# A hybrid trunk layer on one core: x is transposed unnormalised, and its norm is moved to the weights and to V

## The reference, cut to what matters

```
def rmsnorm(x, g):
    return x * rsqrt(mean(x*x, -1) + EPS) * g          # EPS = 1e-6
u   = rmsnorm(h, mix_norm_g)
qkv = u @ wqkv                                         # (1024, 1536)
q, k, v = split(qkv)
q = rmsnorm(q, gq); k = rmsnorm(k, gk)                 # per head, over 64
scores = q k^T / 8 - slope*dist, masked to 128 back, softmax with a sink
h = h + (probs @ v) @ wo
h = h + square(relu(rmsnorm(h, mlp_norm_g) @ w1)) @ w2
h = h + sigmoid(rmsnorm(h, ple_norm_g) @ w_gate) * (p @ w_proj)
```

## Time and profile before

| | us |
|---|---|
| median of 3 runs | 1136.48 (1136.44 to 1138.27) |
| profiled execution | 1134.62 |
| its span | 1132.8 |
| first score product of block 0 starts | 37.03 |
| distance of two blocks in the steady part | 32.77 |
| start of the first product with wo | 270.72 |

### The profile page before, as it was taken

How to read it: one execution, slowest core, us unless ns; L and a number is a source line. 1 busy time by engine, 2 the same in 40 slices (tenths; PEclk the granted TensorE clock), 3 DMA queues, 4 the chain that set the end, 5 groups by cost and what they waited for, 6 DMA issues and landing times.

```text
span 1132.8 us, 15063 instructions
## 1 busy us (share of the span) xinstructions
PE 1102.8 (97%) x5418; PEld 925.4 (82%) x5418; DVE 766.1 (68%) x1170; ACT 453.1 (40%) x796; POOL 116.3 (10%) x191
## 2 busy tenths in 40 slices
PE   7899999998999999899999999999999999999998
PEld 5788888886888887688888888888888888888887
DVE  5788887888553579866776677588778773564311
ACT  5566666666432323223313324453333332243100
POOL 6531332323100000000000000000000000010000
PEclk9999999999999999999999999999999999999999
DMA  7000000004143304433443234999888882111211
GB/s 279 21 19 19 19 19 19 19 26 161 38 141 101 131 18 167 190 126 137 179 167 130 112 142 139 371 413 340 286 297 284 288 279 75 38 38 56 84 44 41
DMA packets 61801, 154.41 MB, mean 136 GB/s; under 512 B 5040, under 2 KB 6064, under 8 KB 61744
## 3 DMA queue, kind: packets, MB, share of 16 engines
q1 hardware_dynamic: 61600, 153.12, 37.8%
q10 hardware_dynamic: 144, 0.52, 0.1%
HBM read 119.55 MB, written 34.08 MB: 136 GB/s over the span
## 4 chain that ended last, share of the span: by engine, by line
PE 80%; DVE 10%; issue 3%; ACT 3%; POOL 2%; DMA 0%; ACTq 0%; DVEq 0%; POOLq 0%
PE pair L2023 24%; PE pair L2003 21%; PE pair L2066 8%; PE pair L1884 7%; PE pair L1756 5%; PE pair L2043 4%; PE pair L1961 3%; ACT probs L859 2%; PE pair L1824 2%; PE pair L2079 2%; PE pair L1795 2%; DVE probs L1260 2%; DVE probs L1278 1%; PE pair L1931 1%; PE pair L1807 1%
## 5 line engine op out<-in xcount | busy, mean ns | idle before, releaser
L2023 PE MATMUL pair<-uT 128*128 128x512 f32 x1176 | 266.7, 389 | 0.0
L2023 PEld LDWEIGHTS pair<-uT 128*128 128x128 f32 x1176 | 220.7, 188 | 45.8
L1086 ACT ACTIVATE uT<-wo_raw 128x1024 fp32r<-128x1024 f32 x63 | 64.3, 1054 | 105.2 <-PE pair L2023 90.3
L1577 DVE TENSOR_TENSOR uT<-wo_raw,uT 128x1024 fp32r<-128x1024 f32 x63 | 74.9, 1221 | 38.8 <-ACT uT L1086 38.8
L1756 PE MATMUL pair<-WA,xT 128*128 128x512 f32 x384 | 95.7, 398 | 1.7 <-DVE kn L1217 0.9
L1884 PE MATMUL pair<-WA,oT 128*128 128x512 f32 x384 | 91.8, 397 | 2.3 <-DVE WA L1336 1.7
L1884 PEld LDWEIGHTS pair<-WA,oT 128*128 128x128 f32 x384 | 72.3, 191 | 17.7 <-issue 1.9
L859 ACT ACTIVATE probs<-probs,nmax 128x257 f32<-128x257 f32 x128 | 63.8, 501 | 52.2 <-DVE nmax L1265 52.0
L1756 PEld LDWEIGHTS pair<-WA,xT 128*128 128x128 f32 x384 | 69.7, 188 | 18.0 <-issue 3.1
L643 POOL TENSOR_SCALAR row_var<-row_ssq 128x1 f32<-128x1 f32 x24 | 4.6, 192 | 718.5 <-ACT hn L987 712.2
L2003 PE MATMUL pair<-WA,WB 128*128 128x512 f32 x312 | 72.8, 389 | 3.3 <-DVE RES L1537 3.3
(11 more groups left out here) (181 smaller groups left out, 1949.6 us busy)
## 6 DMA issues: line engine op xcount, KB each, us to landing
wo_raw<-in_m_w SPq DMA_DIRECT2D x53, 512.0 KB, 6.4
wo_raw<-hid_kept SPq DMA_DIRECT2D x36, 512.0 KB, 4.6
hid_kept<-RES SPq DMA_DIRECT2D x28, 512.0 KB, 2.6
emb<-in_m_w SPq DMA_DIRECT2D x20, 512.0 KB, 6.1
RES<-in_m_w SPq DMA_DIRECT2D x8, 1024.0 KB, 6.5
RES<-in_a_wqkv SPq DMA_DIRECT2D x12, 512.0 KB, 8.9
uT_f<-in_m_w SPq DMA_DIRECT2D x6, 1024.0 KB, 6.7
act_buf<-hid_kept SPq DMA_DIRECT2D x11, 512.0 KB, 4.4
```

What stands on the lines that cost most here:

```text
L1086: nc.scalar.activation(operand(t, which, HI), unit(t, which), ACT.Copy).then_inc(op_hi, 1)
L1577: nc.vector.tensor_tensor(operand(t, which, LO), unit(t, which), operand(t, which, HI).bitcast(F32), ALU.subtract).then_inc(op_ready, 1)
L2023: mm = nc.tensor.matmul(ps[4 * (j % 2) + m][:], operand(t, 0, s)[:, k, m * P:(m + 1) * P], operand(t, 1, r)[:, k, :], start=(g == 0 and k ...
```

## The change

1. x is transposed as it lands. `x_norm` on DVE is gone, and `turn_x` waits for the DMA of x and reads xb. The next load of x waits for the transposes and for the squares.
2. The channel weights are multiplied into wqkv when it is split. The gain is loaded as 8 rows of 128 numbers (instead of 128 copies of 1024), turned by one PE transpose and copied by DVE into mix_col. `hi_unit` and `lo_unit` of the units 0 to 11 are each two instructions of 128x512 with a per-partition scale instead of one of 128x1024.
3. The row factor is applied in `stage_v` (as ACT's scale). For q and k it is left out, and POOL adds one instruction per block (row_eps) so that the EPS in `head_norm` keeps its meaning.
4. `x_squares` and POOL's `x_norm` are for block n+1 and not n+2: the squares stand at the end of ACT's j = 0, POOL's row factor ahead of `head_norm("q0", n + 1)`.
5. The start is in another order, below. Ten units have a place of their own (two of them in ring), so only units 10 and 11 wait for a place. The 34 + 8 warm-up transposes are 11 + 11 + 11.

```
@@ sp
             def load_x(b):
-                sp.wait_ge(xn_ready, b)
+                sp.wait_ge(xT_done, 2 * b)
+                sp.wait_ge(x_squared, b)
...
-                if u >= 8:
-                    sp.wait_ge(w_split, u - 8 + 1)
+                if u >= 10:
+                    sp.wait_ge(w_split, u - 10 + 1)
...
@@ gpsimd
+            pool.memset(gain[:, 0:P], 0.0).then_inc(gain_zero, 1)
...
+            def x_norm(b):
+                stand(pool, x_squared, b + 1)
+                pool.tensor_scalar(row_var[:], row_ssq[:], 1.0 / D, EPS, ALU.mult, ALU.add).then_inc(x_var, 1)
+                pool.wait_ge(x_var, b + 1)
+                pool.tensor_tensor(row_rstd[:], row_var[:], half[:, 0:1], ALU.pow).then_inc(x_rstd, 1)
+                pool.tensor_scalar(row_eps[:], row_var[:], EPS, 1.0, ALU.mult, ALU.mult).then_inc(x_eps, 1)
+                stand(pool, x_eps, b + 1)
...
-            row_norm(x_squared, x_var, x_rstd, 0)
...
+            x_norm(0)
             for h in range(H):
-                if h == 10:
+                if h == 4:
                     head_norm("k", 0)
+                if h == 9:
+                    head_norm("q0", 0)
                 bias_of(h, slice(P, 2 * P), bias_first)
-            head_norm("q0", 0)
-            row_norm(x_squared, x_var, x_rstd, 1)
...
                 if not last:
+                    x_norm(n + 1)
                     head_norm("q0", n + 1)
-                if x_too and not last:
-                    row_norm(x_squared, x_var, x_rstd, n + 2)
@@ scalar
+                    act.wait_ge(mix_ready, 1)
+                    act.wait_ge(wqkv_in(u)[0], 16 * (u // 10 + 1))
+                    for i in range(2):
+                        last_half = nc.scalar.activation(split_to(kind, k, HI)[:, i, :], raw_wqkv(u)[:, i, :], ACT.Copy,
+                                                         scale=mix_col[:, 2 * k + i:2 * k + i + 1])
...
-                    if j == 1 and x_too:
-                        x_squares(n + 2)
+                    if j == 0 and not last:
+                        x_squares(n + 1)
...
-            act.dma_start(gain[:], mix_g.partition_broadcast(P)).then_inc(gain_in, 16)
+            act.wait_ge(gain_zero, 1)
+            act.dma_start(gain[0:KT, 0:P], mix_g.rearrange("(k p) -> k p", p=P)).then_inc(gain_in, 16)
...
-            x_squares(0)
-            hi_unit(0, "kv", 0)
             xT_hi_half(0, 0)
             xT_hi_half(0, 1)
+            hi_unit(0, "kv", 0)
             hi_unit(1, "kv", 1)
+            x_squares(0)
...
-            hi_unit(9, "q8", 1)
             act.wait_ge(scales_ready, 1)
             k_hi_part(0)
+            hi_unit(9, "q8", 1)
+            part_squares("q0", 0)
             hi_unit(10, "q8", 2)
-            part_squares("q0", 0)
             hi_unit(11, "q8", 3)
-            x_squares(1)
@@ vector
+                    for i in range(2):
+                        last_half = nc.vector.scalar_tensor_tensor(
+                            out=dst[:, i, :], in0=raw_wqkv(u)[:, i, :], scalar=mix_col[:, 2 * k + i:2 * k + i + 1],
+                            in1=top[:, i, :].bitcast(F32), op0=ALU.mult, op1=ALU.subtract)
...
-                            dve.wait_ge(bias_first, 1 + H)
+                            dve.wait_ge(bias_first, 1 + G * (j + 1))
...
-            dve.wait_ge(gain_in, 16)
-            x_norm(0)
-            lo_unit(0, "kv", 0)
+            dve.wait_ge(mix_turned, 1)
+            nc.vector.tensor_scalar(mix_col[:], ps[3][:, 0:KT], 1.0, None, ALU.mult).then_inc(mix_ready, 1)
             xT_lo_half(0, 0)
             xT_lo_half(0, 1)
+            lo_unit(0, "kv", 0)
...
             lo_unit(6, "q0", 2)
+            head_scale("k", 0)
             lo_unit(7, "q0", 3)
-            head_scale("k", 0)
...
             lo_unit(10, "q8", 2)
+            head_scale("q0", 0)
             lo_unit(11, "q8", 3)
-            head_scale("q0", 0)
-            x_norm(1)
@@ tensor
-                pe.wait_ge(xn_ready, b + 1)
+                pe.wait_ge(x_in, 16 * (b + 1))
...
-            warm_up(WARM_UP)
+            def turn_mix():
+                pe.wait_ge(gain_in, 16)
+                nc.tensor.transpose(ps[3][:, 0:P], gain[:, 0:P], ident[:]).then_inc(mix_turned, 1)
+            warm_up(WARM_UP // 3)
+            turn_mix()
+            warm_up(WARM_UP // 3)
             turn_x(0)
-            warm_up(WARM_UP // 4)
+            warm_up(WARM_UP // 3)
```

More of the change, by code:

```diff
@@ L135, in trunk_layer @@
         rden = sb("rden", [P, 2, G], F32)
-        sb("to_line", [P, 56], F32)
+        mix_col = sb("mix_col", [P, KT], F32)
+        row_eps = sb("row_eps", [P, 1], F32)
+        sb("to_line", [P, 47], F32)
         in_a = ExitStack()
@@ L255, in row_kept @@
         def row_kept(b):
-            return 16 * ((U_W1 - b + 7) // 8 + 1)
+            return 16 * (3 if b < 2 else 2)
         units = []
@@ L320, in trunk_layer @@
         x_rstd = sem("x_rstd")
-        xn_ready = sem("xn_ready")
+        x_eps = sem("x_eps")
+        gain_zero = sem("gain_zero")
+        mix_turned = sem("mix_turned")
+        mix_ready = sem("mix_ready")
         xT_done = sem("xT_done")
@@ L429, in split_to, with wqkv_in, raw_wqkv @@
                     "proj": lambda: wp_s[:, s, k, :]}[kind]()
+        def wqkv_in(u):
+            return (ring_in[u - 8] if u in (8, 9) else row_moved[u % 10], 16)
+        def raw_wqkv(u):
+            return (ring[:, u - 8, :] if u in (8, 9) else RES[:, u % 10, :]).rearrange("p (k n) -> p k n", k=2)
         def shaped(raw, like):
@@ L645, in row_norm @@
                 pool.tensor_tensor(row_rstd[:], row_var[:], half[:, 0:1], ALU.pow).then_inc(rstd_sem, 1)
+            def x_norm(b):
[5 more added lines that the diff above has]
+                stand(pool, x_eps, b + 1)
             def head_norm(X, b):
                 stand(pool, summed[X], b + 1)
-                pool.tensor_scalar(var[X][:], ssq[X][:], 1.0 / HD, EPS, ALU.mult, ALU.add).then_inc(var_ready[X], 1)
+                pool.tensor_scalar(var[X][:], ssq[X][:], 1.0 / HD, row_eps[:], ALU.mult, ALU.add).then_inc(var_ready[X], 1)
                 pool.wait_ge(var_ready[X], b + 1)
                 pool.tensor_tensor(rstd[X][:], var[X][:], half[:, 0:NH[X]], ALU.pow).then_inc(rstd_ready[X], 1)
-            row_norm(x_squared, x_var, x_rstd, 0)
             pool.memset(vz[:].bitcast(F32), 0.0).then_inc(zeros_ready, 1)
@@ L710, in place_sinks, with body @@
                                    ALU.mult).then_inc(sink_placed, 1)
-            def body(n, x_too=True, last=False):
+            def body(n, last=False):
                 head_norm("q8", n)
@@ L744, in _ @@
                 if j == 1:
+                    x_norm(1)
                     head_norm("q0", 1)
-                    row_norm(x_squared, x_var, x_rstd, 2)
                     place_sinks(0, 3)
@@ L752, in _ @@
                 body(n)
-            body(NB - 2, x_too=False)
+            body(NB - 2)
             body(NB - 1, last=True)
@@ L789, in x_squares @@
                 act.wait_ge(x_in, 16 * (b + 1))
-                wait(act, xT_done, 2 * b)
+                wait(act, x_rstd, b)
                 nc.scalar.activation(xn[:], xb[:], ACT.Square, accum_out=row_ssq[:]).then_inc(x_squared, 1)
@@ L820, in stage_v @@
                 wait(act, v_ready, b)
-                nc.scalar.activation(vnext[:], ps[0][:, KV * HD:2 * KV * HD], ACT.Copy).then_inc(v_staged, 1)
+                act.wait_ge(x_rstd, b + 1)
+                nc.scalar.activation(vnext[:], ps[0][:, KV * HD:2 * KV * HD], ACT.Copy,
+                                     scale=row_rstd[:]).then_inc(v_staged, 1)
             def values(slot, s):
@@ L881, in before, with body @@
                 return (n, j - lag) if j >= lag else (n - 1, j - lag + GROUPS)
-            def body(n, first=False, last=False, x_too=True):
+            def body(n, first=False, last=False):
                 for j in range(GROUPS):
@@ L929, in oT_hi_half @@
                     act.wait_ge(xT_done, 2 * NB)
+                    act.wait_ge(x_squared, NB)
                     act.wait_ge(attended, GROUPS * (b + 1))
@@ L969, in _ @@
                 body(n)
-            body(NB - 2, x_too=False)
-            body(NB - 1, last=True, x_too=False)
+            body(NB - 2)
+            body(NB - 1, last=True)
             oT_hi_half(1, 1)
@@ L1178, in lo_unit @@
             def lo_unit(u, kind, k):
-                raw = RES[:, u % 8, :] if isinstance(u, int) and u < U_W1 else ring[:, k % 2, :]
+                raw = ring[:, k % 2, :]
                 dst, top = split_to(kind, k, LO), split_to(kind, k, HI)
                 dve.wait_ge(w_hi, u + 1)
+                if isinstance(u, int) and u < U_W1:
+                    for i in range(2):
+                        last_half = nc.vector.scalar_tensor_tensor(
+                            out=dst[:, i, :], in0=raw_wqkv(u)[:, i, :], scalar=mix_col[:, 2 * k + i:2 * k + i + 1],
```

(5 more changed lines are left out.)

14 lines of the change are left out of this document (6 added, 8 removed).

## The result

The changed kernel takes 1146.56 us (median, 1143.48 to 1146.92), the kernel before 1136.45 beside it: ratio 1.0082, with a 95% interval of 1.007 to 1.0093. It is slower by 10 us where 1.4 us less were forecast. The profiled execution took 1146.76, its span is 1145.0.

What follows compares the result with a forecast made beforehand. PE's own work was taken to bind the kernel, 97% busy, leaving gains only in the start: 1.3 to 1.6 us at the first group, taken as 1.4, so 1136.48 - 1.4 = 1135.1 us, range 1133.0 to 1137.3.

Steps and rivals of the forecast that it cites:

- the steady blocks: Attention blocks after the start: moved squares, POOL's added instruction and stage_v's scale cost nothing, bounds -0.58 and +0.2 us a block.
- the rest is PE bound and carries it: Everything behind the first group keeps the start's lead of 1.3 to 1.6 us, taken as 1.4.
- the rivals: Four: cheap pairs 1133.5 (0.26), gain given back on DVE 1137.3 (0.13), slow PE 1139.5 (0.07), steady wait gone 1131 (0.04).
- Rival 3: Start: idle PE falls to half pace, 10 us, 7 hidden: 1139.5; against: today's idle stretches are longer, harmless; chance 0.07.
- The last sentence of the prediction: Signs of being wrong: unit 4 at 16.2, changed block length, scores waiting for POOL, another length behind the attention.
- x without its norm: Start: x's transposes no longer wait for the norm, xT split ends about 7.5, not 12.2; PE starts about 2.6 us earlier.
- The gain as 8 rows: Start: dropping the 512 KB broadcast lands everything behind 1.3 us earlier (bounds 0 and 1.6), unit 4 at 14.9.
- The weights scaled in halves: Weight splits: ACT +0.32 us a unit; DVE pair 1.4, +0.17 a unit, 1.4 us over units 4 to 11.
- DVE's queue: Start from unit 4 on: k scaled 2.3 us earlier, from 22.4; q0 scaled 1.5 us earlier, from 31.8.
- POOL's order: Start: seven bias tiles and two sinks behind the q0 factors end about 36; q8 factors asked at 36.6, hidden.
- low part 11: Start, behind the q0 scaling: ends at 33.8; first scores at 35.4, 1.6 us earlier; 1.3 us kept at first bias add.

Runs made afterwards that it cites:

- after_to_line40: The changed kernel with to_line 40 columns wide instead of 47, putting xT, uT and oT back at multiples of 256 bytes: 1134.77 us, ratio 0.9986.
- aligned_warm_longer: The changed kernel with to_line 40, warm-up transposes 5 before x and 29 behind, x's squares behind unit 3, unit 6's high part before k's squares: 1134.5 us, ratio 0.9979.

## Why the prediction was wrong

The sum had a start and then "Sum: nothing" for the steady blocks and "another length of what follows the attention, which nothing here touches" as what can't happen. That is the step that failed, and with it "the rest is PE bound and carries it": PE was bound by its own work, and that work became dearer. I costed the instructions of the diff and not its allocations: the change moves the data tiles by 32 bytes against the weights, a term of 12.1 us, which I had put at nothing. None of the rivals was it. Rival 3, headed "Slower", looked for a slow PE in the clock and in the start. Its event did come in two kernels (after_to_line40 and aligned_warm_longer, eight products each), but in after the products of the start were at full pace, so it has no part in the 10 us. Its reason against also rests on a misreading: the 2.8 us for which PE idled in the kernel before stand ahead of x's transposes, and ahead of the first projection it waited 0.70 us.

```profile
9.59 1.06 PE L1738 MATMUL pair<-ident,xn 128*128 128x128 f32 x8 [2.79 <-DVE xn L1187]
```

The last sentence of the prediction did name the sign, a block's length that changes and another length behind the attention, and both came.

The start, point by point (us; the forecast for wo is 270.72 less the 1.4 of the sum):

| | forecast | after | after_to_line40 |
|---|---|---|---|
| x transposed | 5.1 | 6.94 | 6.41 |
| first projection | 9.6 | 11.93 | 10.94 |
| unit 4, high part | 14.9 | 14.95 | 13.96 |
| k scaled | 22.4 | 21.80 | 21.69 |
| q0 scaled | 31.8 | 31.24 | 31.12 |
| first scores | 35.4 | 34.98 | 34.86 |
| first bias add | 36.6 | 36.44 | 36.30 |
| one block | 32.77 | 32.98 | 32.74 |
| first product with wo | 269.3 | 270.59 | 269.21 |

- *x without its norm*: mis-sized. The transposes stood behind the warm-up, not behind x: the first eleven took 2.61 us, PE waited 0.41 for the gain, the next eleven ran at 0.23 us each, to 7.1. In after, ACT then works without a break from its split of x at 8.03 to unit 4, so the late transposes set that row; what they cost at the end, no run isolates.
- *The gain as 8 rows*: the gain wasn't quite beside the warm-up (PE waited the 0.41 us), but mix_col was ready at 5.0, ahead of unit 0's high part at 9.00; x landed after 3.6 us and no longer 5.1. The forecast of 14.9 for unit 4 was met at 14.95 by luck: it was for a landing, and in after ACT's own queue set that time. Where ACT did wait for the landing, it came at 15.07 and 15.27 (16.21 before), so 0.9 to 1.1 us earlier for the 1.3 that I took; in after_to_line40 it came by 13.96.
- *The weights scaled in halves*: a DVE pair takes 1.41 to 1.46 (forecast 1.4), an ACT pair 1.33 alone (1.38); removing them gave 1.28 us, with the reservation above, of the forecast 1.4.
- *DVE's queue, POOL's order, low part 11*: right to within 0.7 us at every row of the table from unit 4 on; k's factors were there at 21.35, 0.95 before the forecast. The gain at the first bias add is 1.50 (forecast 1.3).
- *The steady blocks*, as far as instructions go: right. 32.74 us with the tiles aligned, the same 0.6 wait. The lead of 1.64 at the first bias add (37.94 - 36.30) was 1.51 at the wo product (270.72 - 269.21).
- With the 32 bytes taken back the change gives 1134.77, 1.6 us less than before (0.6 to 2.5 by the interval), where 1135.1 was forecast. From unit 4 on the mechanism of the forecast was right, ahead of it the steps were late, and the whole gain is some seven times smaller than the loss that it missed.

How the lead went in after, at the same product of each stage (after minus before, us): -1.34 at 56, -0.53 at 186, -0.13 at wo, +1.72 and +2.92 at the next two stages, +9.64 when the contraction begins, +9.67 when it ends, +12.20 at the end. The +9.64 holds 1.6 us that are not the tiles': PE's granted clock fell a second time, behind its 3.2 us gap near 466 us. Windows of after:

```profile
465.00:470.00 5.00, 1.81 (x8) 0.87 0.93 361
470.00:475.00 5.00, 5.00 (x13) 0.50 0.30 125
475.00:480.00 5.00, 5.00 (x22) 0.95 0.49 193
```

after_to_line40 has the same fall in its profile (0.66 from 465 to 470) and the profile of before has not, although PE waits 3.29 us there:

```profile
465.00:470.00 5.00, 3.47 (x15) 1.00 0.39 154
```

So after_to_line40 is 1.50 us ahead of before when the MLP's products begin and 0.13 behind when the contraction begins, which is why their spans are alike (1132.9 and 1132.8) though the medians differ by 1.6.

## What to carry to other kernels

Read a diff's allocations as closely as its instructions: a new tile of one column moved everything behind it, and the unnamed tile there (to_line) was padding whose width kept the operands together. After any such edit, compute the start address of each matmul operand from the compiled program, modulo 256, and compare weights with moving data; here it was worth seven times the change. When a loss shows in stages that an edit doesn't touch, with PE full and its granted clock at 1.00, count matmuls in equal windows and group them by pair of tiles before thinking of the start.

## What the runs showed of the hardware that I had not expected

- Two fp32r operands of a 128x512 product that don't start at the same place within 256 bytes cost some 6 ns a product, 233 for 227 (2.8%), in seven kernels; a common shift of both costs nothing. Shifts of 32, 64 and 128 bytes cost about the same in most pairs; others weren't run.
- PE's half rate can come in the start behind a wait, and the same wait needn't bring it. In after_to_line40, behind 2.29 us of waiting and five products, eight products came 0.40 to 0.43 us apart, at a granted clock of 0.50 (1.2 GHz); in after, behind 2.30 us, none did. What it cost, no run isolates. after_to_line40 was 0.99 us ahead of after at the first projection and at unit 4, and 0.12 ahead at the first scores.

```profile
12.00:13.00 1.00, 1.00 (x5) 0.59 1.04 400
13.00:14.00 1.00, 1.00 (x4) 0.50 1.07 414
14.00:15.00 1.00, 1.00 (x4) 0.50 1.05 406
```

- The transposes alone again doubled their pace, but later: 7 in a us from 5 to 6 us (12 in the earlier trace rows), 11 from 8 to 9, at a recorded clock of 1.00. The Trainium skill (TensorE: Matmul & The Clock Gate, Part 4: PE-mode transpose) says that transposes don't count as activity for the clock; as before, these rows show a pace that rose with nothing but transposes running.
